# Dealing the adaptive modulations' pieces out again over a four-layer kernel

## The reference, cut to what matters

```
mod = jax.nn.silu(c) @ ada_w[i] + ada_b[i]                    # 3 x 1024, i = 0, 1: first block
shift, scale, gate = jnp.split(mod[:, None, :], 3, axis=-1)
h = x * (1.0 + scale) + shift
x = layer_norm(alpha * x + gate * ((y * silu(z)) @ w_out[i]), ...)

mod_l = (jax.nn.silu(c) @ w_ada + b_ada)[:, None, :]          # 6 x 1024, once per hybrid layer
sh1, sc1, g1, sh2, sc2, g2 = jnp.split(mod_l, 6, -1)
hl = rms_norm(xl, norm_mix) * (1.0 + sc1) + sh1
xl = xl + g1 * (concat([att, ml, pool]) @ w_out)
h2l = rms_norm(xl, norm_ffn) * (1.0 + sc2) + sh2
xl = xl + g2 * swiglu(h2l, w_g, w_u, w_d)
```

## Time and profile before

| | |
|---|---|
| time, median of 3 | 2633.34 us |
| profiled execution | 2635.93 us, span 2634.1 us, granted clock 0.906 |
| PE busy | 2220.4 us (84%) |
| DVE busy | 1362.2 us (52%) |
| ACT busy | 906.9 us (34%) |
| chain that ended last | PE 60%, DVE 14%, POOL 10%, DMA 6%, ACT 5% |
| loads of pieces | 24 + 48 of 1024 KB, 8.9 and 6.8 us to landing |

### The profile page before, as it was taken

The page is one execution under the profiler, slowest core; times in us unless marked ns, Lnnn a source line. Parts: engine busy times, 40 slices in busy tenths (PEclk is TensorE's granted clock), DMA queues, the critical chain, the costliest instruction groups (busy, mean ns, idle before and its releaser), DMA issues.

```text
span 2634.1 us, 33814 instructions
## 1 busy us (share of the span) xinstructions
PE 2220.4 (84%) x13593; PEld 1674.5 (64%) x13593; DVE 1362.2 (52%) x2527; ACT 906.9 (34%) x1779; POOL 501.3 (19%) x457
## 2 busy tenths in 40 slices
PE   6878888779899775489788987879999977976998
PEld 5756666558556575389553443668888745545998
DVE  4648677553446999165334355453333223455554
ACT  3335454551212432154212344232222222344443
POOL 0047787311058950000000010000000000000000
PEclk8989999999899987699889987989999978887999
DMA  8254454793344329975322211223323442102553
GB/s 277 92 166 134 133 168 132 231 294 111 128 108 107 84 67 192 235 197 165 110 78 64 80 65 49 64 64 96 96 84 91 146 142 64 65 1 86 178 176 106
DMA packets 423666, 324.38 MB, mean 123 GB/s; under 512 B 65086, under 2 KB 411470, under 8 KB 422358
## 3 DMA queue, kind: packets, MB, share of 16 engines
q1 hardware_dynamic: 386452, 295.70, 38.7%
q10 hardware_dynamic: 34242, 16.92, 2.2%
q0 software_dynamic: 2816, 9.60, 1.1%
HBM read 292.42 MB, written 29.75 MB: 122 GB/s over the span
## 4 chain that ended last, share of the span: by engine, by line
PE 60%; DVE 14%; POOL 10%; DMA 6%; ACT 5%; issue 4%; SPq 1%; ACTq 1%; DVEq 0%; POOLq 0%
PE ps L119 58%; POOL A L88 9%; DVE A L88 3%; ACT A L115 3%; DMA wbuf<-ctab 2%; DVE R L88 2%; DVE A L102 2%; PE ps L122 2%; DVE A L105 1%; DVE A L92 1%; SPq L125 1%; DVE A L93 1%; POOL A L125 1%; DVE A L96 1%; DMA wbuf<-in_ada_w 1%
## 5 line engine op out<-in xcount | busy, mean ns | idle before, releaser
L119 PE MATMUL ps<-R,R 128*128 128x256 f32 (+1 forms) x3968 | 843.8, 335 | 42.6 <-ACT R L115 32.5
L119 PEld LDWEIGHTS ps<-R,R 128*128 128x128 f32 x3968 | 631.9, 194 | 125.5 <-ACT R L115 26.5
L119 PE MATMUL ps<-HR,R 128*128 128x512 f32 (+1 forms) x1984 | 562.4, 368 | 44.4 <-DVE R L88 33.2
L88 DVE TENSOR_TENSOR R<-wbuf,R 128x1024 fp32r<-128x1024 f32 (+2 forms) x304 | 333.0, 1104 | 367.6 <-ACT R L115 367.5
L119 PEld LDWEIGHTS ps<-HR,R 128*128 128x128 f32 x1984 | 354.0, 191 | 110.6 <-issue 43.9
L115 ACT ACTIVATE A<-ps 128x512 f32<-128x512 f32 (+4 forms) x400 | 210.2, 555 | 598.2 <-PE ps L119 422.1
L88 POOL TENSOR_TENSOR A<-A 128x512 f32<-128x512 f32 (+3 forms) x258 | 293.5, 1152 | 568.2 <-DVE A L96 304.3
L88 DVE TENSOR_TENSOR A<-A 128x128 f32<-128x128 f32 (+4 forms) x796 | 361.9, 485 | 63.3 <-ACT A L115 26.7
L115 ACT ACTIVATE R<-wbuf 128x1024 fp32r<-128x1024 f32 (+2 forms) x304 | 270.1, 894 | 293.8 <-PE ps L119 265.7
L119 PE MATMUL ps<-H,wbuf 128*128 128x512 f32 (+2 forms) x928 | 344.1, 530 | 22.1 <-DVE H L93 22.1
L119 PE MATMUL ps<-A 128*128 128x64 f32 (+10 forms) x1736 | 295.7, 371 | 31.1 <-DMA wbuf<-ctab 10.6
(11 more groups left out here) (102 smaller groups left out, 1628.2 us busy)
## 6 DMA issues: line engine op xcount, KB each, us to landing
wbuf<-in_w_ada SPq DMA_DIRECT2D x48, 1024.0 KB, 6.8
wbuf<-in_ada_w SPq DMA_DIRECT2D x24, 1024.0 KB, 8.9
wbuf<-in_w_out SPq DMA_DIRECT2D x24, 1024.0 KB, 5.6
wbuf<-in_w_ffn_gate SPq DMA_DIRECT2D x22, 1024.0 KB, 5.4
wbuf<-in_w_ffn_up SPq DMA_DIRECT2D x22, 1024.0 KB, 5.4
wbuf<-in_w_ffn_down SPq DMA_DIRECT2D x32, 704.0 KB, 4.6
wbuf<-in_attn_w_in SPq DMA_DIRECT2D x20, 1024.0 KB, 7.0
ctab<-A ACTq DMA_DIRECT2D x64, 256.0 KB, 3.0
```

The lines of the kernel that those rows point to most:

```text
L88: return self.op(lambda e: e.tensor_tensor(out, a, b, op))
L119: return self.op(lambda e: e.matmul(out, lhsT, rhs, start=start, stop=stop, skip_group_check=True))
```

## The change

It moves pieces of the modulations and splits the waits for them. Nothing else is computed, and DVE's instructions stay in their order. In the first attention 16 pieces remain of 32: the extra step at `at % 8 == 3` goes, and in the last group only every third step takes a piece. The joint of LN2 gets 2 + 5 pieces, the start of `b0` keeps its 3 but now behind `second_half(rm1)`, `b0`'s `LastHead` gets 2, its joint before the feed-forward 4. At the start of `b1` 3 pieces stay of 10; its filler gets 6, `LastHead` 2 and the joint before the feed-forward the last 2. `ada1` gets piece 7 as a flush, `ada2` and `ada3` pieces 7 and 11; `Mod2`, `rm1`, `HalvesMX` and `rm2` wait for the piece that they need.

```diff
-        ADA = [Ada(f"ada{l}", ..., MODS[l], (7,) if l == 0 else ())
+        ADA = [Ada(f"ada{l}", ..., MODS[l], (7,))
-        ADA += [Ada(f"ada{2 + l}", ..., MODS[2 + l])
+        ADA += [Ada(f"ada{2 + l}", ..., MODS[2 + l], (7, 11))
 # Mod2.dve
-                dve.wait_ge(act_evac, ("ada1", "M"))
+                dve.wait_ge(act_evac, ("ada1", "t", 7))
 # flow, first attention
                     if i < 16 and g < 3:
                         step(proj)
-                    else:
+                    elif g < 3 or i % 3 == 0:
                         step(backlog)
                     if at % 7 in (0, 2, 4, 5):
                         step(tables)
-                    elif at % 8 == 3:
-                        step(backlog)
 # flow, behind S5
             rest(on(GLU))
+            if e.name == "dve":
+                e.wait_ge(act_evac, ("ada1", "M"))
             rest(on(OUT2))
-            rest(on(LN2))
+            ln = on(LN2)
+            step(ln)
+            step(backlog, 2)
+            step(ln)
+            step(backlog, 5)
             e.mark("ctx2")
 # RmsMod.dve2
-                dve.wait_ge(act_evac, (f"ada{2 + l}", "M"))
+                dve.wait_ge(act_evac, self.mod)
 # rm1 and rm2
+        rm1 = RmsMod(N + "m1", ..., x_ready, H, (f"ada{2 + l}", "t", 7))
+        rm2 = RmsMod(N + "m2", ..., HT, (f"ada{2 + l}", "M"))
 # HalvesMX.dve
+                dve.wait_ge(act_evac, (f"ada{2 + l}", "t", 11))
 # Layer flow
             e.mark(N)
-            if l:
-                rest(backlog)
...
             on(rm1)
-            step(backlog, 3 if l == 0 else 0)
             on(second_half(rm1))
+            step(backlog, 3)
...
-                    if i % 3 == 0 and l == 0:
+                    if i % (3 if l == 0 else 4) == 0:
                         step(backlog)
...
             on(LastHead(1))
+            step(backlog, 2)
...
             on(rm2)
             on(second_half(rm2))
+            if l:
+                rest(backlog)
+            else:
+                step(backlog, 4)
```

More of the change, by code:

```diff
@@ L637, in build @@
             dve = pool = none
-        ADA = [Ada(f"ada{l}", I["ada_w"][l], 24, 0, VT[:, 32 + 24 * l:56 + 24 * l], MODS[l], (7,) if l == 0 else ())
+        ADA = [Ada(f"ada{l}", I["ada_w"][l], 24, 0, VT[:, 32 + 24 * l:56 + 24 * l], MODS[l], (7,))
                for l in range(2)]
-        ADA += [Ada(f"ada{2 + l}", I["w_ada_2"][l], 48, 16, VT[:, 128 + 48 * l:176 + 48 * l], MODS[2 + l])
+        ADA += [Ada(f"ada{2 + l}", I["w_ada_2"][l], 48, 16, VT[:, 128 + 48 * l:176 + 48 * l], MODS[2 + l], (7, 11))
                 for l in range(2)]
@@ L2135, in __init__ @@
         class RmsMod:
-            def __init__(self, name, cc, nv, cs, csh, ready, Hd):
+            def __init__(self, name, cc, nv, cs, csh, ready, Hd, mod):
                 self.name, self.cc, self.nv, self.cs, self.csh, self.ready, self.Hd = name, cc, nv, cs, csh, ready, Hd
+                self.mod = mod
             def pe(self, pe):
@@ L2180, in second_half @@
             return Second()
-        rm1 = RmsMod(N + "m1", 0, VT[:, 224 + 8 * l:232 + 8 * l], 8, 0, x_ready, H)
+        rm1 = RmsMod(N + "m1", 0, VT[:, 224 + 8 * l:232 + 8 * l], 8, 0, x_ready, H, (f"ada{2 + l}", "t", 7))
         def h_ready(k):
@@ L2732, in __init__ @@
         HT = AV(4096, 4096, 8)
-        rm2 = RmsMod(N + "m2", c0, VT[:, 240 + 8 * l:248 + 8 * l], 32, 24, lambda k: [(dve_evac, (N + "out", k))], HT)
+        rm2 = RmsMod(N + "m2", c0, VT[:, 240 + 8 * l:248 + 8 * l], 32, 24, lambda k: [(dve_evac, (N + "out", k))], HT,
+                     (f"ada{2 + l}", "M"))
         class HalvesHT:
```

## The result

| | before | after |
|---|---|---|
| median of 4 runs each, interleaved | 2636.37 us (2630.73 to 2643.47) | 2611.26 us (2602.98 to 2612.14) |
| ratio | | 0.9895, 95% interval 0.9876 to 0.9915 |
| profiled execution | 2635.93 us, span 2634.1 us, clock 0.906 | 2602.98 us, span 2601.2 us, clock 0.915 |

The medians differ by 25.1 us; the forecast was 24.4 us and 2609 us. The profiled execution of after is the lowest of its four, and 32.9 us lie between the two spans, so that the profile flatters the change. I therefore ran the changed kernel again later (median 2613.4 us of 6 runs, ratio 0.991 [0.9891, 0.9928]) and read both profiles.

The account below looks back on a forecast made before the run. PE, busy 84% of the span and 60% of the chain, bounds the kernel only where others wait for it; gains and costs at the moved pieces sum to -24.4 us, forecasting 2609 us against the 2633.34 median, range 2602 to 2616.

Parts of the forecast that it names:

- the start of `b1`: From the last residual to DVE's scaling: ACT squares at once, scaling at 2107.1 instead of 2137.43, a gain of 30.3 us.
- The root at `b0`'s start: ACT's root moves ahead of three evacuations, from 1321.15 to 1317.05: a gain of 4.1 us.
- LN2: Two pieces ahead of the squares cost 4.4 us, the fifth behind the sum makes `ctx_2` 0.7 later: cost 5.1 us.
- `b1`'s wait for `ada3`: Joint before `b1`'s feed-forward: DVE waits for the last two pieces, in `MOD` at 2419.2 instead of use at 2416.86; cost 2.3 us.
- The two pieces behind `b1`'s LastHead: They lie beside DVE's reciprocal and root of the head norm: cost nothing, at most 3.1 us.
- the filler of `b1`: Six pieces of 1.54 us in `b1`'s attention and mLSTM, at PE's 60.5% chain share: cost 5.6 us, between 0 and 9.2.
- hidden nearly everywhere: Rival, 20%: pieces in `b1`'s attention cost nothing and the first attention's last group gives 5.4 us; total 2601 us.
- the last attention group: First attention's last group, thinned: 5.4 us at full clock, 3 taken as gain; ends 8 gained, 10 lost.
- the clock swings: Rival, 22%: the first attention's last group loses 3 us instead of gaining 3, `b1`'s six pieces cost 9.2; total 2619 us.
- The flush: Turning a piece in its own step: 0.85 us each where PE is on the path, up to five added.
- `b0`'s filler: It keeps nine pieces, with one flush more: cost 0.5 us.
- The third rival, late panels: Rival, 6%: panels behind moved pieces load late, about 6.8 us each; one or two give 2616 to 2623 us, all seven 2657.

Follow-up runs that it names:

- the first experiment: Kernel before with only `b1`'s start reordered: its ten pieces stand behind `second_half(rm1)`, piece 7 of `ada2` and `ada3` flushed; 2627.15 us, ratio 0.9962.

## Why the prediction was right, and where it was not

The total was right to 2.3 us, with the start of `b1` as the main cause: 31.95 us for 30.3, by the order. 1.65 us more came since it took 8.37 us from the first square to the scaling (2098.75 to 2107.12) and not the 10.1 of the earlier trace rows. The root at `b0`'s start gave 4.1 of 4.1. That the rest came out so near was in part luck: three terms of other stretches were off by 3.5 to 11 us each, with opposite signs.

LN2 cost 6.0 and 6.9 us for 5.1. Its squares came 3.95 us behind the centring where I had 4.9: pieces start 1.54 us apart as in the earlier trace rows, and the flush took less than the earlier trace rows say. But from the first square to the scaling it took 6.76 us instead of 5.43, and the ring held the fifth piece, so that the load of `ctx_2` was issued 1.2 us behind DVE's norm where I had 0.7. The Trainium skill's fit (DMA: Bandwidth & Descriptors, Anatomy of one DMA) had ruled the late fifth piece out; the trace has it late by 1.72 us, and a median load of 5.2 us, between the page's 4.4 and the old row's 6.8. Taking the longer was right: the fifth panel was issued at 1288.49, when its slot came free, and landed at 1294.49, 6.0 us later. `b1`'s wait for `ada3` was 1.6 us for 2.3. The two pieces behind `b1`'s LastHead, costed at nothing, took 0.7 and 0.9 us, and 2.3 us in three other kernels with the same two there (5.61 to 5.62 for 3.35); those in `b0` cost nothing (10.43 for 10.52).

Two steps failed, and they nearly cancel: the first came out 10.7 and 7.5 us better than its term, the second 7.2 and 6.7 us worse. The first is the filler of `b1`, "6 x 1.54 x 0.605 = 5.6 us". PE's share of the chain says what less work on PE would be worth at the same clock; it can't say what more work does to the clock. In ten traces with the six pieces, or with dummies in their place, the stretch from H to the reciprocal is 229.6 to 233.4 us at granted clocks of 0.89 to 0.95 in the attention; in the three with nothing there (before, and the experiments that moved the six pieces to `b0` or gave the first attention its pieces back) it is 234.8 to 236.2, at 0.79 to 0.81. Against the mean of these three, six pieces gave 2 to 6 us back. The rival *hidden nearly everywhere* was right about this place, and too careful. One trace speaks against a plain rule: the first experiment had no pieces in the filler and yet 93.73 us at 0.88 in the attention itself, less than any kernel with pieces. What decides where the clock falls in such an attention stays open; that dummies alone shortened it is shown once, by 3.9 us.

The second is the last attention group, 3 us gained by forecast and 3.7 to 4.2 lost in after. Six thinned traces without dummies have 75.7 to 79.3 us and clocks of 0.74 to 0.82, the one with them 72.41 at 0.93. That is the rival *the clock swings*, for this half of it, with its "+3". The Trainium skill's warning (TensorE: Matmul & The Clock Gate, A second HAM failure mode) agrees with these rows, and so did my own; I gave the clock 2.4 us of the 5.4 where it took more than all. A granted clock under 0.9 in this group was a sign of being wrong in the prediction, and it came: 0.78 in both profiles of after. Had both clock terms been read in the one way, the last group at +3 and the filler at -3, the sum would be 2.6 us lower.

The flush was mis-sized, "0.85 us" each from the earlier trace rows. Before, too, the copy stands behind an exponential that waits for DVE:

```profile
518.55 0.72 ACT L116 ACTIVATE A<-A 128x512 f32<-128x512 f32 x1 [2.44 <-DVE A L92]
```

But two pieces lie on PE in that step (516.45 to 519.11 with the turn between), and cover most of it. With one piece in the step PE waits 1.89 us, and then runs at half clock for some microseconds: 4.3 to 4.7 us each in the full group. `b0`'s filler took 4.0 and 6.6 us more than before where 0.5 was forecast. It has one flush more than before there, but so has the first experiment, at before's time; what makes the difference stays open, since no run removed that flush alone.

The third rival, late panels, did not come at `b1`'s start: the product with H waits for DVE and not for `in_w_in`. The one panel waited for in a changed joint of after was LN2's fifth, 1.72 us. The stall of the earlier trace rows stayed. Both on PE, after:

```profile
506.19 1.94 PE L119 MATMUL ps<-wbuf,CS 128*32 128x256 f32 x16 [6.00 <-DMA wbuf<-in_ada_w]
...
2113.59 6.52 PE L119 MATMUL ps<-H,wbuf 128*128 128x512 f32 x10 [1.72 <-DVE H L93]
```

## What to carry to other kernels

Work that is due later goes behind the instruction that feeds the chain on each in-order engine, not ahead of it: at `b1`'s start ACT's squares stood behind ten evacuations, and their order was worth 32 us there, or 21 with all ten pieces left behind it. Ask of every step that makes an engine wait for another's copy what stands ahead of that copy in the other's program; where a value is needed much later, let the turn ride with the next piece. And price a piece in a latency-bound stretch by several traces of such stretches with and without thin work, clock beside time, not by PE's share of the chain: the same stretch without pieces took 93.7 us in one trace and 101.5 or 101.6 in three.

## What the runs showed of the hardware

More work on TensorE made a stretch shorter: 96 matmuls that nobody reads took 3.9 us off `b1`'s attention (clock 0.81 to 0.89), and with 192 the last attention group took 72.4 us at 0.93 where six profiles without them have 75.7 to 79.3 at 0.74 to 0.82. The kernels with dummies have one profile each, and one attention without any was shorter still (93.73 us at 0.88). A wait of 1.89 us on PE was followed by 6 us at a clock of 0.52, and a full group with two such flushes more took 84 us instead of 75. The same instructions in the same order, S5's, took 556 to 566 us from profile to profile, so that effects of 4 us are seen only in the stage in which they arise.
